# A two-block transformer kernel: who issues the opening transfers, in which pieces, and how many identity matmuls come first

## The reference

```python
h = x
for layer in range(DEPTH):
    hn = rmsnorm(h, mix_norm_g[layer])
    if layer % 2 == 0:
        h = h + even_mixer(hn, ev_w_in[e], ev_conv_w[e], ev_pool_w[e], ev_pool_scale[e], ev_w_out[e])
    ...
# even_mixer starts with
z = h @ w_in                      # 256 x 1024 by 1024 x 2048
...
pool_in = z[..., 3 * A_W:]        # the columns 1536 to 2047
```

## Time and profile before

| what | value |
|---|---|
| median of 3 runs | 1242.11 us (1241.94 to 1242.13) |
| profiled execution, its own time | 1241.86 us |
| its span in the trace | 1240.2 us |
| PE busy | 1226.8 us, 99% of the span |
| DVE, ACT, POOL busy | 967.9, 703.7, 135.2 us |
| first instruction of the head on PE | 13.16 us |

### The profile page before, as it was taken

The page is one execution under the profiler, slowest core; times in us unless marked ns, Lnnn a source line. Parts: engine busy times, 40 slices in busy tenths (PEclk is TensorE's granted clock), DMA queues, the critical chain, the costliest instruction groups (busy, mean ns, idle before and its releaser), DMA issues.

```text
span 1240.2 us, 18559 instructions
## 1 busy us (share of the span) xinstructions
PE 1226.8 (99%) x7013; PEld 1062.9 (86%) x7013; DVE 967.9 (78%) x1218; ACT 703.7 (57%) x1061; POOL 135.2 (11%) x249
## 2 busy tenths in 40 slices
PE   8999999999999999999999999999999999999998
PEld 7989888888778989998889888888888998888887
DVE  5868999977885798898788688997685898676654
ACT  6555555556465555555677566555564243755552
POOL 5000000010000211111132201120010010000000
PEclk9999999999999999999999999999999999999999
DMA  9746777665562798893132348997466597386540
GB/s 325 236 153 218 241 248 238 223 200 180 186 202 68 235 329 311 313 334 115 55 120 71 137 169 293 392 392 261 170 200 208 171 316 259 124 291 212 179 161 34
DMA packets 153649, 265.77 MB, mean 214 GB/s; under 512 B 6092, under 2 KB 110480, under 8 KB 153584
## 3 DMA queue, kind: packets, MB, share of 16 engines
q1 hardware_dynamic: 134560, 204.75, 48.9%
q0 software_dynamic: 18544, 59.65, 13.6%
q10 hardware_dynamic: 480, 0.49, 0.1%
HBM read 263.78 MB, written 1.08 MB: 214 GB/s over the span
## 4 chain that ended last, share of the span: by engine, by line
PE 87%; DVE 8%; ACT 2%; issue 2%; POOL 1%; DMA 0%; POOLq 0%; ACTq 0%; DVEq 0%
PE ps L1949 24%; PE ps L1929 17%; PE ps L1932 9%; PE ps L1915 4%; PE ps L1914 4%; PE ps L1913 4%; DVE w_lo L1142 2%; PE ps L1992 2%; PE ps L1994 2%; PE ps L1993 2%; PE ps L2056 2%; PE ps L1970 2%; PE ps L1972 2%; PE ps L2058 2%; PE ps L1971 2%
## 5 line engine op out<-in xcount | busy, mean ns | idle before, releaser
L1142 DVE TENSOR_TENSOR w_lo<-raw,w_hi 128x2048 fp32r<-128x2048 f32 (+3 forms) x211 | 434.1, 2072 | 32.2 <-ACT w_hi L580 31.9
L580 ACT ACTIVATE w_hi<-raw 128x2048 fp32r<-128x2048 f32 (+3 forms) x213 | 368.7, 1737 | 61.7 <-PE ps L1949 51.1
L1929 PE MATMUL ps<-xn,w_hi 128*128 128x512 f32 x976 | 244.7, 393 | 0.1
L1929 PEld LDWEIGHTS ps<-xn,w_hi 128*128 128x128 f32 x976 | 178.2, 188 | 35.5 <-issue 1.6
L1932 PEld LDWEIGHTS ps<-xn,w_lo 128*128 128x128 f32 x976 | 133.1, 190 | 9.6
L1932 PE MATMUL ps<-xn,w_lo 128*128 128x256 f32 x976 | 136.1, 282 | 0.0
L1949 PE MATMUL ps<-w_hi,a_hi 128*128 128x512 f32 x432 | 134.6, 393 | 0.2 <-DVE a_lo L1854 0.2
L661 ACT ACTIVATE work<-ps 128x512 f32<-128x512 f32 x61 | 36.3, 595 | 171.7 <-PE ps L1932 171.7
L1949 PE MATMUL ps<-w_lo,a_hi 128*128 128x512 f32 x432 | 133.5, 390 | 0.0
L1949 PE MATMUL ps<-w_hi,a_lo 128*128 128x512 f32 x432 | 133.2, 389 | 0.0
L1913 PE MATMUL ps<-xn,w_hi 128*128 128x256 f32 x432 | 122.6, 284 | 0.0
(11 more groups left out here) (362 smaller groups left out, 2006.6 us busy)
## 6 DMA issues: line engine op xcount, KB each, us to landing
raw<-in_ffn_w SPq DMA_DIRECT2D x64, 1024.0 KB, 5.5
side<-in_ada_w POOLq DMA_DIRECT2D x96, 512.0 KB, 6.1
raw<-in_ffn_w_in SPq DMA_DIRECT2D x40, 1024.0 KB, 5.2
raw<-in_ffn_w_out SPq DMA_DIRECT2D x32, 512.0 KB, 5.2
raw<-in_gm_w_in SPq DMA_DIRECT2D x16, 1024.0 KB, 6.4
raw<-in_od_w_in SPq DMA_DIRECT2D x12, 1024.0 KB, 5.5
raw<-in_gm_w_out SPq DMA_DIRECT2D x8, 1024.0 KB, 5.5
raw<-in_ev_w_in SPq DMA_DIRECT2D x7, 1024.0 KB, 13.3
```

What stands on the lines that cost most here:

```text
L580: nc.scalar.activation(w_hi[s][:, 0:w], raw[s][:, 0:w], ACT.Copy).then_inc(hi_done, 1)
L1142: nc.vector.tensor_tensor(w_lo[s][:, 0:w], raw[s][:, 0:w], w_hi[s][:, 0:w].bitcast(F32), ALU.subtract)\
L1929: nc.tensor.matmul(o, hi, xn[:, 512 * k:512 * k + 512], start=k == 0, stop=False)
```

## The change

Five edits, all but the last two in the first 20 us.

1. The five transfers `first_rows` move from ACT's queue to SP's, behind the two halves of the first weight tile and ahead of the second tile.
2. The first 128 tokens of h come in two transfers of 256 KB (columns 0 to 511, then the others). ACT's first square waits for the left one only (`in_left`); DVE waits for both.
3. POOL issues five of its eleven `later_rows` first; the other six (c_ctx, four mla vectors, ada_b) come behind the roots and behind the scaling of the second 128 tokens.
4. The identity is multiplied 7 times instead of 11 before the wait for `in_rows`.
5. One semaphore of the attention part (`neg`) is dropped and its increment is counted on `f`, which is then waited for at 2 instead of 1.

```diff
+        in_left = sem("in_left")
...
             for t in range(TT):
-                sp.dma_start(h[:, t, :], x_v[:, t, :]).then_inc(in_h[t], 16)
+                if t == 0:
+                    sp.dma_start(h[:, 0, 0:512], x_v[:, 0, 0:512]).then_inc(in_left, 16)
+                    sp.dma_start(h[:, 0, 512:], x_v[:, 0, 512:]).then_inc(in_h[0], 16)
+                else:
+                    sp.dma_start(h[:, t, :], x_v[:, t, :]).then_inc(in_h[t], 16)
...
                 sp.dma_start(dst, kview(ev_w)[:, 2 * m:2 * m + 2, 1536:2048]).then_inc(full, 16)
+            for r, p, m, src in first_rows:
+                sp.dma_start(stage[p:p + m, r, :], src).then_inc(in_rows, 16)
             for t in range(T_EV + 1, T_FFN0):
                 load(t)
...
             act.dma_start(ident, I["consts"][:, 0:P]).then_inc(in_id, 16)
-            for r, p, m, src in first_rows:
-                act.dma_start(stage[p:p + m, r, :], src).then_inc(in_rows, 16)
             act.dma_start(cst[:, P:], I["consts"][:, P:C_ALL]).then_inc(in_cst, 16)
...
-                        act.wait_ge(in_h[t], 16)
+                        act.wait_ge(in_left if (t, c) == (0, 0) else in_h[t], 16)
...
+            dve.wait_ge(in_left, 16)
             dve.wait_ge(in_h[0], 16)
             half_scale("ev", 0)
...
-            nc.vector.tensor_tensor(zf[:, 3, :], zf[:, 1, :], zf[:, 2, :], ALU.subtract).then_inc(AT["neg"], 1)
+            nc.vector.tensor_tensor(zf[:, 3, :], zf[:, 1, :], zf[:, 2, :], ALU.subtract).then_inc(AT["f"], 1)
...
-            dve.wait_ge(AT["f"], 1)
+            dve.wait_ge(AT["f"], 2)
...
             pe.wait_ge(in_id, 16)
-            for _ in range(11):
+            for _ in range(7):
                 nc.tensor.matmul(ps[7][:, 0:P], ident, ident, start=True, stop=True)
...
-                    pe.wait_ge(AT["neg"], 1)
+                    pe.wait_ge(AT["f"], 1)
...
-            pe.wait_ge(AT["f"], 1)
+            pe.wait_ge(AT["f"], 2)
...
-            for r, p, m, src in later_rows:
+            for r, p, m, src in later_rows[:5]:
                 pool.dma_start(stage[p:p + m, r, :], src).then_inc(in_later, 16)
...
                     .then_inc(hs_ready, 1)
+            for r, p, m, src in later_rows[5:]:
+                pool.dma_start(stage[p:p + m, r, :], src).then_inc(in_later, 16)
             chain(nc.gpsimd.memset(rel[:, :], 1.0))
```

More of the change, by code:

```diff
@@ L379, in build @@
         RELU = [group(f"relu{n}", "sq", "ahi", "a_ready") for n in range(2)]
-        AT = group("at", "qk", "v_sb", "v_act", "z_ps", "zt", "z", "nabs", "ez", "ln", "neg", "f_ps", "f", "sel", "s_ps", "s_sb",
+        AT = group("at", "qk", "v_sb", "v_act", "z_ps", "zt", "z", "nabs", "ez", "ln", "f_ps", "f", "sel", "s_ps", "s_sb",
                    "max", "exp", "p", "t_ps", "pt", "o_ps", "ohi", "a_ready")
```

## The result

The changed kernel takes 1244.86 us, median of 13 runs (1244.14 to 1245.85), against 1241.90 for the kernel before on the same chips (1241.69 to 1242.68): 2.96 us or 0.24% slower, ratio 1.0024 with a 95% interval of 1.0016 to 1.0031. The forecast was 1243.3, range 1241.7 to 1244.9. The sign and the place were right, the size was not: the loss is two and a half times the forecast 1.2, and the median lies 0.04 us inside the upper end of the range. The profiled execution took 1244.94 us with a span of 1243.3, 3.1 more than before.

What follows compares the result with a forecast made beforehand. PE bounds the kernel from 31 us on, so opening delays carry to the end; block 6 hangs on PE and DVE. PE's +1.2 us, covering the other terms, gives 1243.3 us, range 1241.7 to 1244.9.

Steps and rivals of the forecast that it cites:

- the low clock: Rival in PE's opening: clock stays low through the fillers, +2.5 us, up to +3.3 with late rows; 18%.
- a stall at the second vec_rows: Sign of a wrong forecast: PE waiting for ada_b between the head's halves; no such wait was forecast.
- The frame: Block 6 on PE follows rows' copy + 8.3 us and second tile's landing + 4.9, meeting within 0.1 us.
- Rows behind the first tile: On SP's queue the rows land at 10.9 us, bounds 10.0 to 11.3; DVE's copy 0.9 late.
- The rows add 0.17: On SP's queue the rows land 0.17 us after the first tile's second half, at 10.9.
- The step before it: On SP's queue the first tile's second half lands 0.3 us earlier, at 10.75.
- Fewer warm-ups: PE's warm-ups end at 8.3 us, PE idles 2.6 until 10.9; three clock cases: +0.6, +2.5 or +1.2.
- the second option: PE's clock needs another 5.5 us of work after the gap: head at 16.0, block 6 +2.5 us.
- the third option: Work before PE's gap counts: level up at 13.2, head at 14.6, block 6 +1.2 us; the case taken.
- POOL's last six rows: Behind POOL's scaling, ada_b is issued at 15.3 us and lands at 21.1, between 20.4 and 21.9, in time.
- h in two transfers: In the opening, DVE's scaling starts near 6.9, 1.7 us earlier, worth nothing; the extra 0.4 issue on SP hides.
- The sum: Block 6 is 1.2 us late, bound by PE; DVE's +0.6 and ada_b's landing are covered: 1243.3 us.

Runs made afterwards that it cites:

- b_rows_sp: Kernel before with only the five first rows moved to SP's queue behind the first tile's halves: 1243.68 us, +1.80 against before.
- b_split: Kernel before with only h's first 128 tokens in two transfers and the attention semaphores merged: 1242.91 us, +1.03 against before.
- a_warm24: Changed kernel with 24 identity matmuls instead of 7 ahead of the rows: 1243.84 us, +1.96 against before.
- b_warm7: Kernel before with only the identity matmuls ahead of the rows cut from 11 to 7: 1242.52 us, +0.52 against before.
- b_pool: Kernel before with only POOL's six later rows moved behind its scaling: 1243.10 us, +1.22 against before.
- a_later_ahead: Changed kernel with all eleven later rows issued first again by POOL: 1245.31 us, +3.13 against before.
- a_warm11: Changed kernel with 11 identity matmuls instead of 7 ahead of the rows: 1244.76 us, +2.58 against before.
- a_rows_act: Changed kernel with the five first rows back on ACT's queue, between identity and constants: 1243.27 us, +1.09 against before.

## Why the prediction was right in sign and short in size

- **The range held by luck.** Its upper end was put at 1244.9 to take in half of the low clock. The measured 1244.86 got there by three sizes that were all short. Up to the second half the forecast was +1.2 and the trace has +2.78. The 1.6 between them is 0.65 for the rows (11.55 for 10.9), 0.5 for the clock (4.2 us from rows to head for 3.7), 0.65 for the wait for ada_b (forecast none) and 0.1 for the transposes behind it, less 0.3 that PE took back in the head. The forecast's own narrow range, 1242.8 to 1243.9, was missed. So was the forecast's picture: head at 15.7 and not between 14 and 15, and a stall at the second vec_rows, one of its own signs of being wrong.
- **The frame held.** A delay of the opening is carried to the end (table, last column), and block 6 hangs on the copy of the rows and on the second tile. `b_rows_sp` moves the first leg (copy +1.69, block 6 +1.36, second half +1.19; 0.3 was given back, as forecast), `b_split` the second (tile +1.02, second half +1.01).
- **Rows behind the first tile: right mechanism, mis-sized.** I had them at 10.9, bounds 10.0 to 11.3. They landed at 11.5 in the changed kernel, 11.7 to 12.5 in four other profiles with the same order, outside the bounds in all five. The step that failed is "The rows add 0.17". The step before it held: the second half landed at about 2.7 + 8.1 = 10.8, for the forecast 10.75. But the rows came 0.7 behind it, and 64 KB by the transfer rate alone don't explain that; what does isn't shown. DVE's copy was 1.49 late instead of 0.9.
- **Fewer warm-ups: between two of the three.** I let the 3.2 us of work before the gap count and put the level up at 13.2. The granted clock was 0.50 until 15.2. The head started at 15.7, which looks like the 16.0 of the second option, but over half of its 1.1 us beyond my 14.6 is the late rows. From the rows to the head it took 4.2 us, where the third option had 3.7 and the second 5.1. `a_warm24` measured 1.0 us less without the gap, an earlier ada_b included; `b_warm7`, where the rows are not moved, lost 0.73 in its profile and 0.5 in the median, not clear of no change. The trace of before gave one rise after unbroken work and no case of a gap; between two ends I took the middle without a row for it.
- **POOL's last six rows: mis-sized, outside its bounds.** Forecast 21.1, bounds 20.4 to 21.9, half a microsecond in time; measured 22.84, 0.65 late. Of the 1.7, scaling started 1.1 later than I had it (10.63, since h's second part came at 8.17 rather than 7.2) and ran 4.14 instead of 3.25, 0.9 more; issue to landing took 5.4, 0.4 less than I had. `b_pool` shows the edit costs 1.2 by itself. What it costs in the changed kernel stays open: without it (`a_later_ahead`) the time was no better, but the rows landed later in that profile.
- **h in two transfers: costed at nothing, wrong.** I named its cover on PE and DVE (and DVE's scaling came at 8.38, hardly the 6.9 I gave it), but looked only at who waits for h, not at what lands behind it. Alone it measured 1.0, through the second tile. In the changed kernel that tile landed at 13.7 as before, and the split has no cost of its own in the trace.
- **The sum.** The edits alone give 1.80 + 1.03 + 1.22 + 0.52 = 4.6, together they give 2.96: several of them are floors under the same time stamp and cover one another. That later rows first do not help the changed kernel, with 7 or 11 warm-ups (+0.17 and +0.41 between medians), is not settled; in the one profile of each the rows landed later, by 1.0 and by 0.3.

## What to carry to other kernels

Here five small transfers moved off one engine's queue and behind 2 MB on another. That freed 2.4 us of issuing, which no engine on the critical chain needed, and cost 1.8 us of landing (9.9 to 11.7 in `b_rows_sp`), which PE and DVE waited for. Ask of each small transfer what stands ahead of it in its new queue and who waits. In these runs a dummy matmul was worth its time as long as PE would otherwise have stood idle before a stretch of short matmuls; shorten the warm-up only if the wait behind it gets shorter too, and look at the durations behind it. And before costing an opening edit by edit, find the last common time stamp; edits that hold it up singly do not add.

## What was not expected of the hardware

- After a gap of 3.2 us behind 3.4 us of work, the granted clock fell to 0.50 at 11.8, just after the work had resumed at 11.55, and stayed there until 15.2 through unbroken work. After a gap of 1.7 us behind 5.06 us of work (`b_rows_sp`) it did not. Of this the Trainium skill (TensorE: Matmul & The Clock Gate, Part 1: The HAM clock gate) says that the slow level is the default and activity lifts it; these traces agree: the warm-ups began at 0.23 us each and the same instruction took 0.11 after unbroken work. The record has the fall at the moment the work resumes, not during the gap.
- The granted clock read 1.00 from the start of every trace, also while warm-ups ran at 0.23 us, twice their later time. It also read 1.00 while the fillers of `b_warm7` took 0.19 each. So the column can miss a low level that lasts from the start; the durations have to be read beside it.
- GpSimd's scaling of the same 128 x 1024 values took 3.11 to 4.81 us in these profiles, and 3.12 and 4.14 in two kernels that differ only in PE's warm-ups (`a_warm11` and the changed one).
- Splitting one 512 KB transfer in two went with 191 GB/s in a slice that had 285, and with a landing 1.0 us later for the second weight tile, in the two kernels that left the five rows on ACT's queue (`b_split`, `a_rows_act`). With the rows behind the first tile and POOL's six rows late, the tile was in time in spite of the split (13.7 in the changed kernel).
